# Stick-breaking attention summed by parts

## What is computed

```
logits = einsum('bqhd,bkhd->bhqk', q, k) * 64 ** -0.5
mask = key_pos < q_pos
log_keep = where(mask, log_sigmoid(-logits), 0.0)
later = lax.cumsum(log_keep, axis=3, reverse=True) - log_keep
weights = where(mask, exp(log_sigmoid(logits) + later), 0.0)
out = einsum('bhqk,bkhd->bqhd', weights, v)
```

## Time and profile before

| | us |
|---|---|
| median of three runs | 2292.34 (2290.48 to 2293.79) |
| profiled execution, its own time | 2289.84 |
| its span, first to last instruction | 2288.0 |
| TensorE busy | 2228.6 (97%) |
| VectorE busy | 1525.7 (67%) |
| GpSimd busy | 1213.5 (53%) |
| ScalarE busy | 1083.4 (47%) |

### The profile page before, as it was taken

The page is one execution under the profiler, slowest core; times in us unless marked ns, Lnnn a source line. Parts: engine busy times, 40 slices in busy tenths (PEclk is TensorE's granted clock), DMA queues, the critical chain, the costliest instruction groups (busy, mean ns, idle before and its releaser), DMA issues.

```text
span 2288.0 us, 31164 instructions
## 1 busy us (share of the span) xinstructions
PE 2228.6 (97%) x11281; PEld 1769.6 (77%) x11281; DVE 1525.7 (67%) x1961; ACT 1083.4 (47%) x1966; POOL 1213.5 (53%) x792
## 2 busy tenths in 40 slices
PE   9999989999999999999999989998999999999999
PEld 6778867677878888888887756676778888888886
DVE  7865768776597554689439966566686575545745
ACT  5554157675364555444446366554222342225653
POOL 2212145444257666657767355544457795556663
PEclk9999999999999999999999999998999999999999
DMA  4113353344325443855452300011311543348554
GB/s 160 38 45 99 120 179 109 98 127 168 111 89 193 159 153 135 308 172 166 150 170 83 120 19 29 28 47 51 111 65 56 183 153 125 111 136 291 184 171 147
DMA packets 153764, 289.43 MB, mean 126 GB/s; under 512 B 34915, under 2 KB 44387, under 8 KB 153612
## 3 DMA queue, kind: packets, MB, share of 16 engines
q1 hardware_dynamic: 153612, 287.44, 38.0%
HBM read 207.88 MB, written 79.51 MB: 126 GB/s over the span
## 4 chain that ended last, share of the span: by engine, by line
PE 87%; DVE 5%; ACT 3%; POOL 2%; issue 2%; DMA 1%; SPq 0%; DVEq 0%; POOLq 0%; ACTq 0%
PE bank L861 15%; PE bank L865 15%; PE bank L863 15%; PE bank L633 10%; PE bank L637 10%; PE bank L635 10%; PE bank L710 2%; ACT t L1000 2%; PE bank L940 2%; PE bank L927 2%; PE bank L958 1%; POOL t L2063 1%; PE bank L830 1%; POOL t L2179 1%; PE bank L848 1%
## 5 line engine op out<-in xcount | busy, mean ns | idle before, releaser
L2063 POOL TENSOR_TENSOR t<-t,t 128x512 fp32r<-128x512 f32 (+1 forms) x539 | 861.8, 1610 | 805.9 <-ACT t L1000 787.0
L1000 ACT ACTIVATE t<-t 128x512 fp32r<-128x512 f32 (+2 forms) x734 | 468.8, 662 | 754.1 <-PE bank L865 351.3
L861 PE MATMUL bank<-t,t 128*128 128x512 f32 x1568 | 614.5, 392 | 5.4 <-DVE t L1797 4.6
L865 PE MATMUL bank<-t,t 128*128 128x512 f32 x1568 | 611.1, 390 | 0.9 <-DVE t L1425 0.9
L863 PE MATMUL bank<-t,t 128*128 128x512 f32 x1568 | 611.2, 390 | 0.0
L633 PE MATMUL bank<-t,t 128*128 128x512 f32 x1072 | 431.0, 402 | 0.2 <-ACT t L1000 0.2
L637 PE MATMUL bank<-t,t 128*128 128x512 f32 x1072 | 418.9, 391 | 1.3 <-DVE t L1425 0.7
L635 PE MATMUL bank<-t,t 128*128 128x512 f32 x1072 | 418.1, 390 | 1.5 <-POOL t L2063 1.5
L861 PEld LDWEIGHTS bank<-t,t 128*128 128x128 f32 x1568 | 295.0, 188 | 68.6 <-DVE t L1797 5.0
L865 PEld LDWEIGHTS bank<-t,t 128*128 128x128 f32 x1568 | 295.0, 188 | 63.4 <-DVE t L1425 1.7
L863 PEld LDWEIGHTS bank<-t,t 128*128 128x128 f32 x1568 | 295.1, 188 | 62.4 <-issue 1.0
(11 more groups left out here) (244 smaller groups left out, 2532.4 us busy)
## 6 DMA issues: line engine op xcount, KB each, us to landing
t<-in_w SPq DMA_DIRECT2D x87, 512.0 KB, 3.5
hid_scr<-t SPq DMA_DIRECT2D x112, 256.0 KB, 2.1
t<-hid_scr SPq DMA_DIRECT2D x112, 256.0 KB, 2.7
t<-in_wf SPq DMA_DIRECT2D x80, 256.0 KB, 3.2
t<-in_wf SPq DMA_DIRECT2D x36, 512.0 KB, 4.1
g_scr<-t SPq DMA_DIRECT2D x36, 512.0 KB, 2.9
t<-g_scr SPq DMA_DIRECT2D x72, 256.0 KB, 3.5
t<-in_wo SPq DMA_DIRECT2D x24, 512.0 KB, 3.6
```

The costliest lines, as they stand in the source:

```text
L861: e.matmul(ps, hi, XH, start=start, stop=False)
L865: return e.matmul(ps, hi, XL, start=False, stop=stop)
L1000: return e.activation(out, in_, ACT.Copy, **kw)
L2063: return e.tensor_tensor(out, x, high.bitcast(F32), ALU.subtract)
```

## The change

The mask now adds +1e30 (tile `farq`), so keep = sigmoid(−logit) is 0 where the key is not before the query, and `sg` is one ACTIVATE from the bank. The scan computes state = keep · state + z. z is a new tile `zr` with zeros and, in its last 128 columns, the identity: it sets P to 1 at the query's own position. `st` transposes the suffix products from `keep`, which `sg` now may overwrite only after `st` of the block two before. The sum by parts is: sum of w[t] v[t] = v[query] + sum of P[t] (v[t−1] − v[t]). GpSimd makes the differences (`vd`, two instructions for each pair, one tile of 4 KB a partition), `vt` transposes them instead of the values. The values go to `yS` directly and `so` adds the bank to them, so `sv` leaves the ring of stage tiles. The tiles `odds` go.

```diff
-        self.odds, self.keep = many(169, 4, 2, [128, 2, 512]), [many(177 + 8 * a, 4, 2, [128, S]) for a in range(2)]
+        self.vd, self.zr, self.keep = at(169, [128, S]), at(173, [128, 512]), [many(177 + 8 * a, 4, 2, [128, S]) for a in range(2)]
...
     def vt(i, g):
         ps = tr_bank("vt", i, g)
-        q.wait_ge(*[done("evd", B.at["sv", i, f]) for f in range(2)])
-        transposes(ps, M.stage[B.stg["sv", i] % 3], g).then_inc(*tick("vt", i, g))
+        q.wait_ge(done("vd", i))
+        transposes(ps, M.vd, g).then_inc(*tick("vt", i, g))
...
     def st(i, qb, g):
-        q.wait_ge(done("sw", 0, i, p_), done("sw", 1, i, p_))
+        q.wait_ge(done("ss", 0, i, p_), done("ss", 1, i, p_))
...
-                last = e.transpose(ps[:, o:o + 128], M.odds[a][:, p_ % 2, k:k + 128], ident)
+                last = e.transpose(ps[:, o:o + 128], M.keep[a][qb % 2][:, k:k + 128], ident)
...
     def sg(a, i, p_):
         qb, k0, k1 = PIECES[p_]
-        n, odds = 12 * i + p_, M.odds[a][:, p_ % 2, 0:k1 - k0]
+        z = banks[2 + 2 * a + p_ % 2][:, 0:k1 - k0]
         q.wait_ge(done("sl", i, p_))
...
-        e.activation(odds, banks[2 + 2 * a + p_ % 2][:, 0:k1 - k0], ACT.Sigmoid).then_inc(*tick("sg", a, i, p_))
-        q.wait_ge(part("sg", (a, i, p_), 1))
         if i or qb >= 2:
             i0, qb0 = (i, qb - 2) if qb >= 2 else (i - 1, qb + 6)
-            q.wait_ge(*[done("sw", a, i0, p0) for p0, piece in enumerate(PIECES) if piece[0] == qb0])
-        e.activation(M.keep[a][qb % 2][:, k0:k1], odds, ACT.Identity, scale=-1.0, bias=one_c).then_inc(*tick("sg", a, i, p_))
+            q.wait_ge(*[done("st", i0, qb0, g) for g in range(qb0 // 2 + 1)])
+        e.activation(M.keep[a][qb % 2][:, k0:k1], z, ACT.Sigmoid, scale=-1.0).then_inc(*tick("sg", a, i, p_))
...
+        elif j.kind == "sv":
+            if j.arg >= 2:
+                q.wait_ge(done("s_out", j.arg - 2))
+            else:
+                q.wait_ge(*[done(*x) for x in (K.p3_out if j.arg else K.p3_end)])
+            e.tensor_copy(M.yS[j.arg % 2][:, c], ps[:, :]).then_inc(*tick("evd", b))
...
     def ss(a, i, p_):
+        own = k1 == 128 * (qb + 1)
         x = keep[:, k0:k1][:, ::-1]
-        start = keep[:, k1:k1 + 1] if k1 < 128 * (qb + 1) else 1.0
-        e.tensor_tensor_scan(x, x, one_c.broadcast_to([128, k1 - k0]), start, ALU.mult, ALU.mult).then_inc(*tick("ss", a, i, p_))
+        z = M.zr[:, 512 - (k1 - k0):512][:, ::-1] if own else M.zr[:, 0:1].broadcast_to([128, k1 - k0])
+        start = 0.0 if own else keep[:, k1:k1 + 1]
+        e.tensor_tensor_scan(x, x, z, start, ALU.mult, ALU.add).then_inc(*tick("ss", a, i, p_))
...
     def so(i, qb):
-        e.tensor_copy(M.yS[i % 2][:, 128 * qb:128 * qb + 128], banks[7][:, 0:128]).then_inc(*tick("so", i, qb))
+        q.wait_ge(*[done("evd", B.at["sv", i, f]) for f in range(2)])
+        y = M.yS[i % 2][:, 128 * qb:128 * qb + 128]
+        tt(y, banks[7][:, 0:128], y, ALU.add).then_inc(*tick("so", i, qb))
...
-    def sw(a, i, p_):
-        qb, k0, k1 = PIECES[p_]
-        n = min(k1, 128 * qb + 127) - k0
-        odds = M.odds[a][:, p_ % 2, 0:n]
-        q.wait_ge(done("ss", a, i, p_))
-        e.tensor_tensor(odds, odds, M.keep[a][qb % 2][:, k0 + 1:k0 + 1 + n], ALU.mult).then_inc(*tick("sw", a, i, p_))
+    def vd(i):
+        y = M.yS[i % 2]
+        q.wait_ge(*[done("evd", B.at["sv", i, f]) for f in range(2)])
+        q.wait_ge(done("zr"))
+        if i:
+            q.wait_ge(done("vt", i - 1, 0), done("vt", i - 1, 1))
+        e.tensor_tensor(M.vd[:, 0:1], M.zr[:, 0:1], y[:, 0:1], ALU.subtract)
+        e.tensor_tensor(M.vd[:, 1:S], y[:, 0:S - 1], y[:, 1:S], ALU.subtract).then_inc(*tick("vd", i))
```

More of the change, by code:

```diff
@@ L603, in __init__ @@
         self.whole = o
-        self.stg = {k: n for n, k in enumerate([k for k in seen if k[0] not in ("sq", "sk")])}
+        self.stg = {k: n for n, k in enumerate([k for k in seen if k[0] not in ("sq", "sk", "sv")])}
     def evacuations(self, b):
@@ L920, in sl @@
         if n >= 2:
-            q.wait_ge(*[part("sg", (a, *K.piece_before(n, 2)), 1) for a in range(2)])
+            q.wait_ge(*[done("sg", a, *K.piece_before(n, 2)) for a in range(2)])
         q.wait_ge(*[done("evd", B.at[k, i, f]) for k in ("sq", "sk") for f in range(2)])
@@ L1305, in mask @@
         copy(M.mask[0][:, :], C("ident"))
-        copy(M.mask[1][:, :], C("negq")).then_inc(*tick("mask"))
+        copy(M.mask[1][:, :], C("farq")).then_inc(*tick("mask"))
     def vc(i, g):
@@ L1700, in evd @@
             ts(M.pairs[j.arg % 2][j.kind[1]][:, c], ps[:, :], 0.125 if j.kind == "sq" else 1.0, None, ALU.mult).then_inc(*tick("evd", b))
-        elif j.kind in ("sv", "sg", "pg", "cg"):
+        elif j.kind == "sv":
[4 more added lines that the diff above has]
+            e.tensor_copy(M.yS[j.arg % 2][:, c], ps[:, :]).then_inc(*tick("evd", b))
+        elif j.kind in ("sg", "pg", "cg"):
             n = B.stg[j.kind, j.arg]
@@ L1940, in ss, with zr @@
         keep = M.keep[a][qb % 2]
-        q.wait_ge(done("sg", a, i, p_))
+        q.wait_ge(done("sg", a, i, p_), done("zr"))
         if k1 < 128 * (qb + 1):
             q.wait_ge(done("ss", a, i, p_ - 1))
+        own = k1 == 128 * (qb + 1)
         x = keep[:, k0:k1][:, ::-1]
-        start = keep[:, k1:k1 + 1] if k1 < 128 * (qb + 1) else 1.0
-        e.tensor_tensor_scan(x, x, one_c.broadcast_to([128, k1 - k0]), start, ALU.mult, ALU.mult).then_inc(*tick("ss", a, i, p_))
+        z = M.zr[:, 512 - (k1 - k0):512][:, ::-1] if own else M.zr[:, 0:1].broadcast_to([128, k1 - k0])
+        start = 0.0 if own else keep[:, k1:k1 + 1]
+        e.tensor_tensor_scan(x, x, z, start, ALU.mult, ALU.add).then_inc(*tick("ss", a, i, p_))
+    def zr():
+        q.wait_ge(*[done(*x) for x in K.p3_end])
+        q.wait_ge(done("c1"))
+        e.memset(M.zr[:, 0:384], 0.0)
+        e.tensor_copy(M.zr[:, 384:512], ident).then_inc(*tick("zr"))
     def so(i, qb):
         q.wait_ge(done("sv", i, K.piece_of(qb, 0)))
[L1950 to L1953, removed]
-        e.tensor_copy(M.yS[i % 2][:, 128 * qb:128 * qb + 128], banks[7][:, 0:128]).then_inc(*tick("so", i, qb))
+        q.wait_ge(*[done("evd", B.at["sv", i, f]) for f in range(2)])
+        y = M.yS[i % 2][:, 128 * qb:128 * qb + 128]
+        tt(y, banks[7][:, 0:128], y, ALU.add).then_inc(*tick("so", i, qb))
     def whole(k, f):
@@ L2782, in stage_freed @@
         kind, i = self.stage_keys[n - 3]
-        return [{"cx": ("cz", i), "gc": ("zx", i), "gb": ("yg", i), "pv": ("pf", i), "sv": ("vc", i, 1)}.get(kind, ("g_out", kind, i))]
+        return [{"cx": ("cz", i), "gc": ("zx", i), "gb": ("yg", i), "pv": ("pf", i)}.get(kind, ("g_out", kind, i))]
     def branch_at(self, h, x):
@@ L2869, in signals @@
     return g
[L2872 removed]
+PARTS = dict(mp=0, fsq=2, wc=2, nr=2, kr=2, gb=5, ebx=2, gr=2, fr=2, qx=2, na=2, nc=2, gq=2, cv=4, gc=5, gd=2, lmul=2, sol=2, lex=2, zi=2, ge=2, kk_in=4, gS=2, inv_out=4, inv_in=2, as1=2, as2=2, cz=3, pf=2)
 PARTS["or"] = 2
@@ L3115, in second_layer @@
     add("act", "mask")
+    add("dve", "zr", rank=4)
     add("sp", "plw")
@@ L3148, in second_layer @@
     for i in range(4):
+        add("pool", "vd", i, rank=3)
         for g in range(2):
@@ L3156, in second_layer @@
                 add("dve", "ss", a, i, p_, rank=4)
-                add("pool", "sw", a, i, p_, rank=4)
             for g in K.groups(p_):
@@ L3300, in constants @@
     c["neg1"] = np.where(t <= s, 0, NEG).astype(f)
-    c["negq"] = np.where(t < s, 0, NEG).astype(f)
+    c["farq"] = np.where(t < s, 0, -NEG).astype(f)
     c["own32"] = (s // 32 == t // 32).astype(f)
```

10 lines of the change are left out of this document (3 added, 7 removed), and 4 rows, old and new, of the table SIGNALS.

## The result

| | before | after |
|---|---|---|
| median | 2293.07 us (4 runs, 2290.48 to 2293.83) | 2269.57 us (4 runs, 2266.15 to 2272.68) |
| profiled execution, its own time | 2289.84 us | 2272.68 us |
| its span | 2288.0 us | 2270.9 us |

The ratio is 0.9898 (95% interval 0.9885 to 0.9910): 23.5 us faster. A second set of four runs gave 2269.74 us and 0.9898 again (0.9884 to 0.9913). The forecast was 2274 us, 17.9 off.

What follows compares the result with a forecast made beforehand. TensorE, busy nearly the whole span, bounds the kernel. A ceiling of 24.4 us less 4 of remaining waits and 2.5 at the handover gives 17.9 off 2292.3, so 2274 us (2268 to 2279 at 0.68; ends 2268 and 2283).

Steps and rivals of the forecast that it cites:

- the two places: Attention, 1340 to 1380 and 1560 to 1600 us: TensorE idle 7.1 and 8.4 us, clock 0.91 and 0.83.
- signs that I named: In the attention: TensorE idle under 8 us, clock 1.00, scans 95 to 100 us; at gp one 2 to 3 us wait.
- one sign of being wrong: VectorE's scans in the attention: a scan of 512 exceeding 2 us would show the forecast wrong.
- Ceiling, 24.4 us: TensorE in the attention: 16.6 us of idle time and 7.8 us of half-speed clock go if nothing waits.
- Left over, 4 us: Waits remaining in the attention, 1.8, 0.7 and 1.5 us, taken as 4 us, with 2.5 and 10.4 as ends.
- Handover, 2.5 us: Start of gp behind P4's last bulk matmul: new wait for GpSimd's first weight split, 2.5 us idle, no clock drop.
- From profile to median: Whole execution: the profiled 2289.84 us lay 2.5 us under the median, 2292.34; forecast median 2292.3 − 17.9 = 2274 us.
- Second tile, 0: The scan's second input on VectorE: expected to cost 0, with 0.69 us for each of 64 scans as the end.
- By distance it does too: A piece's logits to its first transposes: at least 5.8 us of TensorE's own work against a 3.3 us chain.
- by load it does: Attention, per head pair: VectorE's 23 us of scans and ScalarE's 23.8 us fit beside TensorE's 34.6 us.
- Rival 3: All four attention pairs stall 10.4 us each if scans exceed 2.3 us or GpSimd locks one out: 2312 us; chance 0.05.
- Rival 1: Attention: only GpSimd's share goes, ScalarE's copy waits stay: 10 us off, 2282 us; chance 0.19 together with another rival.

Runs made afterwards that it cites:

- the corners: Four kernels, long or short chain in old or new TensorE order: stretch 351.3 us (before), 345.6 (chain alone), 359.5 (order alone), 328.9 (both).
- rotated: Changed kernel, but gp's weights begin with the tile freed first instead of the one the last bulk matmul reads: 2267.0 us, 0.9884 of the kernel before.
- act_chain: Changed kernel, TensorE's list held, with only ScalarE's second operation put back between sigmoid and scan: 2279.8 us, 0.9943 of the kernel before.
- company: Changed kernel, TensorE's list held, plus a GpSimd product behind each scan into a scratch tile, no transposes waiting: 2282.3 us, 0.9954 of the kernel before.
- act_company: Changed kernel, TensorE's list held, plus 96 ScalarE ACTIVATEs behind the sigmoids into a scratch tile, nothing waiting: 2267.9 us, 0.9890 of the kernel before.

## Why the prediction was right, and where not

**The direction and the mechanism held.** Of the waits in the two places 1.9 us are left, all in pair 0, and the half clock in them went; TensorE's waits for GpSimd in the chain are gone; with either operation put back they, or their like, return. What the prediction did not part, the corners show: the chain alone gives 5.7 us, and the 22.4 come only with chain and order together. Most signs that I named came out: idle time under 8 us (3.4 before the handover), clock 1.00, scans 98.6 us (95 to 100 said), the last weighted sum 16 us before the last bulk matmul. The wait at the start of `gp` came out as two of 1.6 us together, not one of 2 to 3. And one sign of being wrong, a scan of 512 over 2 us, is there in 3 of the 48 (3.1 to 3.3 us, beside GpSimd); the median is 1.26 us.

**The size was 5 us too small.** 17.9 forecast, 22.4 in the stretch, 23.5 in the medians.

- *Ceiling, 24.4 us.* It counted a wait at its idle time. rotated prices this: two waits with 0.72 + 0.86 = 1.6 us of idle time leave, and 2.2 us go from the stretch. The matmuls overlap, and a wait also ends that:

```profile
1567.64 0.49 PE L861 MATMUL bank<-t,t 128*128 128x512 f32 x1 [0.72 <-ACT t L1000]
...
1568.99 0.50 PE L863 MATMUL bank<-t,t 128*128 128x512 f32 x1 [0.86 <-POOL t L2071]
```

  The second starts 1.35 us behind the first; where nothing waits, these matmuls start 0.23 us apart. So 1.12 us are lost, 0.26 more than the 0.86 shown as idle. At the transposes it is 0.14: a single one is shown as 0.27 us, four in a row take 0.66, so they start 0.13 apart. Rows 2 count 20 waits, two small ones come with them, and 6 are left: 16 at 0.14 to 0.26 each, an estimate from these two prices, are 2.2 to 4.2 us. The sum was 24.4 − 5.0 = 19.4 with the waits as measured; 3.0 are missing to 22.4, and this term is of that size. That it is all of the 3.0 is not shown. The Trainium skill (Perfetto Trace Analysis, Tensor Engine Instruction (MATMUL, LD_WEIGHTS)) says that the reported end of a matmul is an estimate from its size; the 0.39 us shown for matmuls 0.23 us apart agree. The idle time counted from such an end is short by the difference.
- *Left over, 4 us.* Measured 3.4, and term by term: 1.25 for the copy behind a whole weight tile (1.8 said), 0.69 for the last weighted sum of pair 0 (0.7), 1.4 for GpSimd's company (1.5, with no wait for vd). That last one can be read:

```profile
1329.62 3.71 DVE L1949 TENSOR_TENSOR_SCAN t<-t,t 128x512 f32<-128x512 f32 x2
1329.70 2.82 POOL L2189 TENSOR_TENSOR t<-t 128x1023 f32<-128x1023 f32 x1
...
1333.56 0.66 PE L958 MATMUL bank<-t,t 128*64 128x128 f32 x8 [1.23 <-DVE t L1962]
```

- *Handover, 2.5 us.* 0.72 + 0.86 = 1.6. The mechanism was right: ScalarE's copy, then GpSimd's split, into the tile that the last matmul read. From the end of that matmul (1566.92) to the second of `gp` 2.1 us pass, 2.45 forecast; and in them runs the first of `gp`, 0.49 us, which I had left inside the wait. The clock held, as taken. (The second stretch of rows 10 ends where the wait of 2.08 us ends and so doesn't show what came after it; the trace has 1.00 from 1706 to 1712 us too.)
- *From profile to median.* I set the sum against the profiled execution and took its distance to the median as fixed. It was the one execution of the fourteen profiled here that came first to L892, so the profile's 17.1 us matched my 17.9 by chance.
- *Second tile, 0.* Right: 1.26 us alone against 1.28. The Trainium skill (DVE: opcode table, instruction layouts, handler registers and perf-mode slots, Datapath and trigger behaviour) says that this scan runs at half throughput because its result goes back to an earlier stage; a scan of 512 at 1.26 us beside a subtraction of 512 at 0.69 agrees.

**Two steps were weaker than they read.** "By distance it does too" looked only from logits to transposes, 5.8 us. act_chain's chain of about 4.7 us fits in that, and still lost 9.6 us, six times at the logits two pieces on, whose bank a late sigmoid holds. And "by load it does" had VectorE at 23 us a pair; company took it to 35 and lost 12, with VectorE full where most of the waits lay. Both margins were there with the short chain and without GpSimd, as forecast; but they are thinner than the text says. The 195 bulk matmuls that it gives for pair 3 before are 159 of P4 and 36 of `gp`, so the tail was not wholly bare; and pair 0, which it leaves out, got denser too (72 bulk matmuls before, 48 after). Rival 3's condition (GpSimd beside the scans of every piece) is what company sets up, and it costs 3 us a pair, not 10.4.

**Rival 1** put 7.9 us on ScalarE's single bank and freed only GpSimd's share. Its picture is the old order: there the short chain leaves 9.2 to 9.4 us of these waits. My argument against it, that the new order parts the sets, is borne out: in the new order 2.0 us of them are left.

## What to carry over

Cut a chain where another order can use it, and measure both together: here the shorter chain alone gave 6 us, the denser order alone lost 8, and together they gained 22. Before pricing an operation that goes, ask whether it stood in the chain or only on the engine: 59 us of ScalarE beside the chain cost nothing, the same 59 us in it 10. A GpSimd instruction that TensorE doesn't wait for is not free if VectorE scans beside it. And when a wait only moves on to the next instruction, look for what both hang on.

## What the runs showed of the hardware

- GpSimd's company stretched scans of 512 from 1.26 to 1.84 us in the mean (47 of 48 in company), and GpSimd's own operations took 1.41 us in the mean over all sizes, against 1.18 for the products of the kernel before.
- A wait cost TensorE 0.14 us (at transposes) to 0.26 us (at matmuls of 128x512) more than the idle time shown, by the start-to-start times above.
- The same unchanged first 1215 us differ by up to 5.4 us between executions, in part by the time at 1.2 GHz in them (17.1 us in act_company, 27.3 after). A difference of two profiles' spans carries that.
